# Moving attention and gate projections within the first layer's matmul order, with its bias and input loads, on one NeuronCore

## The chip, the cores and the metric

The kernel runs on one NeuronCore of a Trainium2 chip. The metric is the device time of one execution in microseconds (us). Before the change three runs gave a median of 3324.24 us, from 3323.4 to 3331.55.

## The reference

Two transformer-like layers over 512 tokens of width 1024, all in float32. The change lies wholly in the first part of the first one:

```python
h = rmsnorm(x, norm_mix_pre[i])
z = h @ w_in[i]
xr, gr, q, kc, vc, ksl, vsl, kw, vw, g_nsa, gm_rnn, gm_attn = jnp.split(z, IN_SPLITS, axis=-1)
xr = causal_conv(xr, conv_w[i], conv_b[i])
y_rnn = rg_lru(xr, ...) * jax.nn.gelu(gr)
kc_c = compress(kc.reshape(kv_shape), cmp_pos_k[i], cmp_k_w1[i], cmp_k_w2[i])
vc_c = compress(vc.reshape(kv_shape), cmp_pos_v[i], cmp_v_w1[i], cmp_v_w2[i])
y_attn = nsa(q, kc_c, vc_c, ksl..., vsl..., kw..., vw..., g_nsa, slopes)
y = jax.nn.sigmoid(gm_rnn) * y_rnn + jax.nn.sigmoid(gm_attn) * y_attn
x = x + rmsnorm(y @ w_out[i], norm_mix_post[i])
```

`rg_lru` is a gated linear recurrence over the tokens. `nsa` is attention with three branches: a softmax over 31 compressed blocks of keys, one over selected blocks and one over a window; with 512 tokens the last two are both plain causal attention here. After this come a feed-forward layer, an embedding term, and a second block with window attention and a mixture of experts, which the change leaves alone.

## The kernel before

Activations stand transposed: features on 128 partitions, 512 tokens along the free axis, eight such tiles for the width of 1024. One projection (`project`, L159) makes one output tile of 128x512 in one of PSUM's eight banks from eight matmuls. Each float32 matmul shows as two rows in the trace.

All weights come through a ring of six slots in SBUF (`Ring`). `chunk_list` gives the order of the chunks, some 2 MB each (1.5 MB for the recurrence). `feed` issues loads on SyncE's queue up to a given chunk; a load into a slot waits until the chunk that was there has been used (`used` names the semaphore). `take` makes an engine wait for the chunk's landing. Since SyncE issues in program order, everything behind a waiting load waits too.

The program is a row of blocks (`nc.Block`). In a block each engine has a list of instructions of its own, ordered by the code as written and synchronised by semaphores; at the block's end all engines meet at a barrier, SyncE too. The blocks that matter here, in order:

1. `norm_and_start`: SyncE loads x in two halves, two constants, and then feeds six chunks. Its next block, `rms_norms`, squares x on ScalarE, averages on TensorE, and scales on VectorE into H.
2. `recurrent_mixer`: for each of eight tiles three projections of H, and one tile later two gate matmuls (L301, L302) from VectorE's convolution. ScalarE and VectorE work on the recurrence of the tile. At the end TensorE has only the last two gate matmuls, and then ScalarE and VectorE finish the last tile.
3. `attention_inputs`: four projections for the compression's inputs (kc, vc), four for the keys, the values (L446), the 48 gate columns (L454), eight query projections, then the two compressions (L469), each over blocks that VectorE builds in one buffer (L549; the second build waits until the first product has read it), and the small second products.
4. `compressed_probs`: TensorE makes scores for four tiles (L584). VectorE adds a bias that SyncE loads piece by piece into two buffers, takes the maximum, ScalarE applies Exp, and VectorE masks, sums and scales (L603 to L625). TensorE turns the result (L591) and VectorE copies it (L629).
5. `causal_attention`: 32 units, pipelined over TensorE, VectorE and ScalarE. Its sixteen biases come into three buffers, the first three at its start (L702).
6. `mixer_output`: eight projections of H give the attention's gates; ScalarE applies Sigmoid (L846), VectorE multiplies and adds into Y; then eight projections of Y with w_out.

In 3, 4 and 6 the semaphore z_read counts what ScalarE has copied out of the banks, and TensorE waits for it before it writes a bank again.

## Time and profile before

| what | value |
|---|---|
| profiled execution, own time | 3322.41 us |
| its span | 3320.6 us |
| median of three runs | 3324.24 us (3323.4 to 3331.55) |
| TensorE busy | 2893.3 us, 87% of the span |
| VectorE busy | 1028.5 us, 31% |
| ScalarE busy | 673.2 us, 20% |
| moved by DMA | 635.62 MB, 191 GB/s on average |
| granted TensorE clock, mean | 0.932 |

The span runs from the first to the last instruction of the program; the execution's own time lies 1.8 us above it. Busy time says little by itself, since each stage has another limit. The views used below are: the timeline, which lists an engine's instructions in order of time, merged, with the start, the length and, in brackets, the idle time before and what ended it; windows, with the busy time of each engine in a stretch and the granted clock of TensorE (1.00 is 2.4 GHz, 0.50 is 1.2 GHz); and the landing time of DMAs. PE is TensorE, PEld its weight loads, DVE VectorE, ACT ScalarE, SP SyncE; a name with q behind it is that engine's sequencer, which at the end of a block means the barrier.

### The profile page before, as it was taken

The page shows a single profiled execution, that of the slowest core. Times are in us where ns is not written, and L with a number is a line of the kernel's source. Part 1 is how long each engine was busy: PE and PEld are TensorE (multiplying, and loading weights), DVE is VectorE, ACT ScalarE, POOL GpSimd, SP SyncE. Part 2 cuts the span into 40 slices and gives each one's busy share as a digit, 9 for nine tenths or more (in the row PEclk, how much of TensorE's full clock was granted, in tenths as well). Part 3 has the DMA queues.
Part 4 walks back from the last instruction along what each step waited for, and adds up shares of the span by engine and source line. Part 5 has one row for each costly group of instructions (what it writes and reads, how often), then busy time and mean ns, then how long its engine had stood idle before and what let it go on. Part 6 is the DMA issues. An engine that isn't in the chain of part 4 may idle for free. (4 is left out here: it accounts for less than half of the span.)

```text
span 3320.6 us, 37273 instructions
## 1 busy us (share of the span) xinstructions
PE 2893.3 (87%) x14080; PEld 1591.7 (48%) x14081; DVE 1028.5 (31%) x2150; ACT 673.2 (20%) x1368; POOL 123.5 (4%) x185
## 2 busy tenths in 40 slices
PE   6979878997999998898985989988678976999995
PEld 3435556543444443556653545444444643555543
DVE  2330066306788302125343111111322533111113
ACT  2440158311000000115331000000131631000002
POOL 0000000000000000000001001000100001110100
PEclk9989979998999998998996999999789997999997
DMA  4222210026665421111015999999712026999993
GB/s 168 94 80 89 85 53 27 29 76 171 263 228 213 180 82 38 63 51 58 25 54 202 396 406 410 420 401 410 286 50 96 1 82 256 397 391 415 396 403 116
DMA packets 139751, 635.62 MB, mean 191 GB/s; under 512 B 19366, under 2 KB 33062, under 8 KB 88576
## 3 DMA queue, kind: packets, MB, share of 16 engines
q1 hardware_dynamic: 95296, 422.13, 33.6%
q10 hardware_dynamic: 34992, 191.12, 14.3%
q0 software_dynamic: 9360, 21.00, 1.8%
q8 instruction: 65, 1.06, 0.1%
q14 instruction: 38, 0.31, 0.0%
HBM read 615.31 MB, written 37.22 MB: 197 GB/s over the span
## 5 line engine op out<-in xcount | busy, mean ns | idle before, releaser
L159 PE MATMUL psum<-normed,weight_ring 128*128 128x512 f32 x1472 | 642.2, 598 | 36.3 <-PEq L193 17.8
L159 PEld LDWEIGHTS psum<-normed,weight_ring 128*128 128x128 f32 x1472 | 282.5, 192 | 392.9 <-issue 392.9
L2079 PE MATMUL psum<-weight_ring,slot_rows_turned 128*64 128x256 f32 x3456 | 396.8, 383 | 0.9 <-issue 0.9
L2079 PEld LDWEIGHTS psum<-weight_ring,slot_rows_turned 128*64 128x64 f32 x3456 | 246.5, 138 | 146.6 <-issue 32.6
L2079 PE MATMUL psum<-third_stream_weights,slot_rows_turned 128*64 128x256 f32 x1728 | 217.5, 409 | 59.2 <-DMA third_stream_weights<-in_w_dram 59.2
L936 DVE SCALAR_TENSOR_TENSOR psum<-weight_ring,condition_rows 128x1024 f32<-128x1024 f32 x192 | 236.8, 1233 | 15.4 <-issue 0.9
L159 PE MATMUL psum<-modulated,weight_ring 128*128 128x384 f32 (+2 forms) x640 | 228.7, 518 | 0.0
L2079 PEld LDWEIGHTS psum<-third_stream_weights,slot_rows_turned 128*64 128x64 f32 x1728 | 130.3, 148 | 145.8 <-DMA third_stream_weights<-in_w_dram 66.5
L2094 PE MATMUL psum<-weight_ring,expert_hidden_turned 128*64 128x512 f32 x864 | 197.2, 598 | 0.0
L2211 DVE COPY expert_hidden_turned<-psum 128x256 f32<-128x256 f32 x81 | 34.4, 425 | 512.8 <-PE psum L2087 512.8
L2202 DVE COPY slot_rows_turned<-psum 128x512 f32<-128x512 f32 x81 | 56.1, 692 | 397.9 <-PE psum L2058 397.9
L159 PEld LDWEIGHTS psum<-modulated,weight_ring 128*128 128x128 f32 x640 | 121.4, 190 | 105.5 <-issue 51.0
L2155 ACT ACTIVATE expert_silu<-psum 128x256 f32<-128x256 f32 x79 | 30.3, 383 | 614.9 <-PE psum L2079 614.9
L159 PE MATMUL psum<-ffn_hidden,weight_ring 128*128 128x512 f32 x352 | 151.3, 592 | 0.9 <-issue 0.9
L159 PE MATMUL psum<-mix,weight_ring 128*128 128x512 f32 (+1 forms) x384 | 138.0, 521 | 2.2 <-PEq L1362 2.2
L2162 ACT COPY expert_rows<-psum 128x512 f32<-128x512 f32 x81 | 47.4, 585 | 325.2 <-PE psum L2094 325.2
L159 PEld LDWEIGHTS psum<-ffn_hidden,weight_ring 128*128 128x128 f32 x352 | 66.8, 190 | 85.4 <-issue 85.4
L2094 PEld LDWEIGHTS psum<-weight_ring,expert_hidden_turned 128*64 128x64 f32 x864 | 57.4, 136 | 99.1 <-issue 92.5
L159 PEld LDWEIGHTS psum<-mix,weight_ring 128*128 128x128 f32 x384 | 72.8, 190 | 66.7 <-issue 63.4
L2094 PE MATMUL psum<-third_stream_weights,expert_hidden_turned 128*64 128x512 f32 x432 | 98.7, 598 | 1.1 <-DVE expert_hidden_turned L2211 1.1
L1172 PE MATMUL psum<-weight_ring,modulated 128*128 128x384 f32 (+1 forms) x192 | 60.2, 478 | 26.2 <-PEq L1555 17.0
L2058 PE MATMUL psum<-identity,slot_rows 128*128 128x128 f32 x324 | 61.9, 315 | 21.9 <-DMA slot_rows<-token_rows,slot_index 20.1
(359 smaller groups left out, 2896.4 us busy)
## 6 DMA issues: line engine op xcount, KB each, us to landing
weight_ring<-in_w_dram SPq DMA_DIRECT2D x114, 2048.0 KB, 14.5
third_stream_weights<-in_w_dram ACTq DMA_DIRECT2D x81, 2048.0 KB, 18.7
weight_ring<-in_w_ada_dram SPq DMA_DIRECT2D x24, 2048.0 KB, 10.2
weight_ring<-in_w_ffn_dram SPq DMA_DIRECT2D x11, 2048.0 KB, 7.7
expert_rows<-expert_rows ACTq DMA_DIRECT2D x162, 128.0 KB, 12.7
weight_ring<-in_w_rnn_dram SPq DMA_DIRECT2D x8, 1536.0 KB, 14.5
weight_ring<-in_w_att_dram SPq DMA_DIRECT2D x6, 2048.0 KB, 7.6
weight_ring<-in_w_in_dram SPq DMA_DIRECT2D x6, 2048.0 KB, 9.5
```

The costliest lines, as they stand in the source:

```text
L159: last = nc.tensor.matmul(out, weights[:, k * P:(k + 1) * P], rhs(k), start=(k == 0), stop=(k == tiles - 1))
L936: last = nc.vector.scalar_tensor_tensor(out=product, in0=w[:, t], scalar=1.0, in1=CR[:, v, :], op0=ALU.mult, op1=ALU.mult, accum_out=c.mod ...
L1172: last = nc.tensor.matmul(ps[:, 4 + i % 2, 0:n], HX[:, k, i * P:(i + 1) * P], w[:, k, 0:n], start=(k == 0), stop=(k == KT - 1))
L2058: last = nc.tensor.transpose(ps[:, 0, k * P:(k + 1) * P], XS[:, b, k::4], c.ident[:, :])
L2079: last = nc.tensor.matmul(ps[64 * o:64 * o + 64, 2 + b, 256 * m:256 * (m + 1)], XT[:, b, k % 4, 64 * (k // 4):64 * (k // 4) + 64], w[:, k, ...
L2094: last = nc.tensor.matmul(ps[64 * o:64 * o + 64, 5 + b, :], HT[:, b, j % 2, 64 * (j // 2):64 * (j // 2) + 64], w[:, j, 512 * o:512 * (o + 1)],
L2155: nc.scalar.activation(SG[:, b, :], ps[:, 2 + b, 0:256], ACT.Silu).then_inc(silu.sem, 1)
L2162: nc.scalar.copy(YS[:, b, :], ps[:, 5 + b, :]).then_inc(y_copied.sem, 1)
L2202: v.tensor_copy(XT[:, b, :, :].rearrange("p k s -> p (k s)"), ps[:, 0, :]).then_inc(x_copied.sem, 1)
L2211: v.tensor_copy(HT[:, b, :, :].rearrange("p k s -> p (k s)"), ps[:, 1, 0:256])\
```

## The change

It does five things. The waits for both halves of x are put on SyncE ahead of the first ring loads. The four projections of chunk 8 (kc and vc) move from the head of `attention_inputs` into the end of the recurrence's block. The first compression moves between the two groups of four query projections, and the chunk order with it. Four of the eight gate projections move from `mixer_output` into `compressed_probs`, behind the scores; their sigmoids are written over their own weights in the ring slot, which stays in use until `mixer_output` has read it; the scores' banks now take the turned probabilities. The compressed bias is loaded in one piece into the place of the scores, and the first three causal biases are loaded in `compressed_probs`; the ring's next three loads go from `attention_inputs` to the head of `causal_attention`.

```diff
@@ norm_and_start, sync
                 for dst, src in c.const_loads:
                     sp.dma_start(dst, src).then_inc(c.consts_landed, 16)
+                for landed in c.x_landed:
+                    sp.wait_ge(landed, 16)
                 c.ring.feed(sp, Ring.SLOTS)
@@ recurrent_mixer, tensor, behind the loop
+                w = ring.take(pe).rearrange("p (s w) -> p s w", s=4)
+                for u in range(4):
+                    pe.wait_ge(z_read, 3 * KT - 5 + u)
+                    project(nc, ps[:, u, :], w[:, u], lambda k: H[:, k, :]).then_inc(c.att_z_ready, 1)
+                ring.used(c.att_z_ready, 4)
@@ attention_inputs, tensor
-                u = 0
-                for chunk in range(2):
-                    w = ring.take(pe).rearrange("p (s w) -> p s w", s=4)
-                    for s in range(4):
...
+                u = 4
+                w = ring.take(pe).rearrange("p (s w) -> p s w", s=4)
+                for s in range(4):
...
-                for b in range(2):
+                    b = chunk
                     w = ring.take(pe).rearrange("p (l n) -> p l n", l=16)
                     pe.wait_ge(xb_ready, b + 1)
@@ attention_inputs, sync
-                ring.feed(sp, 8 + 6)
                 sp.wait_ge(z_read, 4)
...
-                ring.feed(sp, ring.uses + Ring.SLOTS)
+                ring.feed(sp, ring.uses + 3)
@@ compressed_probs, sync
+                sp.dma_start(PC[:, :, :], c.ios["cmp_bias"]).then_inc(bias_in, 16)
                 sp.dma_start(MASK[:, :, :], c.ios["cmp_mask"]).then_inc(mask_in, 16)
-                for i in range(ST):
-                    if i >= 2:
-                        sp.wait_ge(bias_used, i - 1)
-                    sp.dma_start(BIAS[:, i % 2, :], c.ios["cmp_bias"][:, i, :]).then_inc(bias_in, 16)
-                    sp.wait_ge(bias_in, 16 * (i + 1))
+                for h in range(3):
+                    sp.dma_start(c.bias[:, h, :], c.ios["causal_bias"][h]).then_inc(c.bias_in[h], 16)
@@ compressed_probs, tensor
+                c.early_chunk = ring.uses
+                c.early_gates = ring.take(pe)
...
                     last.then_inc(s_ready, 1)
+                gates_w = c.early_gates.rearrange("p (s w) -> p s w", s=4)
+                for u in range(4):
+                    project(nc, ps[:, 4 + u, :], gates_w[:, u], lambda k: H[:, k, :]).then_inc(c.gm_ready, 1)
                 pe.wait_ge(p_ready, 1)
@@ compressed_probs, vector and scalar
-                    v.tensor_tensor(part, ps[:, i, :], BIAS[:, i % 2, :], ALU.add).then_inc(bias_used, 1)
+                    v.tensor_tensor(part, ps[:, i, :], part, ALU.add)
...
+                act.wait_ge(c.gm_ready, 4)
+                for u in range(4):
+                    nc.scalar.activation(c.early_gates[:, u * S:(u + 1) * S], ps[:, 4 + u, :], ACT.Sigmoid)
@@ causal_attention, sync
-                for h in range(NHEAD):
-                    if h >= 3:
-                        m_ready.wait(sp, ((h - 3) // 2 * UNITS + UNITS - 1) * 4 + (2 if (h - 3) % 2 == 0 else 4))
+                ring.feed(sp, c.early_chunk + Ring.SLOTS)
+                for h in range(3, NHEAD):
+                    m_ready.wait(sp, ((h - 3) // 2 * UNITS + UNITS - 1) * 4 + (2 if (h - 3) % 2 == 0 else 4))
@@ mixer_output, tensor and vector
-                for u in range(2 * KT):
+                for u in range(4, 2 * KT):
...
+                    gate = GA[:, u % 2, :] if u >= 4 else c.early_gates[:, u * S:(u + 1) * S]
...
+                ring.used(y_ready, 4, n=c.early_chunk)
@@ chunk_list
-    out += [tiles("w_att", 8, 4), tiles("w_att", 12, 4)]
-    out += [ios["cmp_k_w1"].rearrange("(l p) n -> p l n", p=P), ios["cmp_v_w1"].rearrange("(l p) n -> p l n", p=P)]
+    out += [tiles("w_att", 8, 4), ios["cmp_k_w1"].rearrange("(l p) n -> p l n", p=P)]
+    out += [tiles("w_att", 12, 4), ios["cmp_v_w1"].rearrange("(l p) n -> p l n", p=P)]
```

TensorE from the last gate matmuls of the recurrence to the second products of the compression, before (each row is a line of the kernel, the operation, its output and inputs and how often; a branch ends or begins a block):

```order
L302 MATMUL psum<-xr_conv,lru_gates_w 128x512
L278 UNCONDITIONAL_BRANCH
L431 UNCONDITIONAL_BRANCH
L159 MATMUL psum<-normed,weight_ring 128x512 x64
L446 MATMUL psum<-weight_ring,normed 128x512 x32
L454 MATMUL psum<-gate_columns,normed 128x48 x32
L159 MATMUL psum<-normed,weight_ring 128x512 x64
L469 MATMUL psum<-cmp_blocks,weight_ring 128x128 x64
```

The same place in the changed kernel:

```order
L304 MATMUL psum<-xr_conv,lru_gates_w 128x512
L159 MATMUL psum<-normed,weight_ring 128x512 x32
L280 UNCONDITIONAL_BRANCH
L438 UNCONDITIONAL_BRANCH
L159 MATMUL psum<-normed,weight_ring 128x512 x32
L452 MATMUL psum<-weight_ring,normed 128x512 x32
L460 MATMUL psum<-gate_columns,normed 128x48 x32
L159 MATMUL psum<-normed,weight_ring 128x512 x32
L475 MATMUL psum<-cmp_blocks,weight_ring 128x128 x32
L159 MATMUL psum<-normed,weight_ring 128x512 x32
L475 MATMUL psum<-cmp_blocks,weight_ring 128x128 x32
```

32 matmuls, four projections, now stand ahead of the block's end, and the first compression stands between the two halves of the query projections.

TensorE from the compressed scores to the causal attention, in the changed kernel; before, the row of L159 is not there and the other rows are the same:

```order
L587 MATMUL psum<-cmp_keys,queries 128x64 x32
L159 MATMUL psum<-normed,weight_ring 128x512 x32
L597 MATMUL psum<-identity,cmp_probs 128x128 x16
L570 UNCONDITIONAL_BRANCH
L712 UNCONDITIONAL_BRANCH
```

Four projections now stand between the scores and the transposes that wait for VectorE.

SyncE's DMAs from the end of `attention_inputs` on, in the changed kernel:

```order
L103 DMA weight_ring<-in_w_att_dram 128x4x1024 x2
L103 DMA weight_ring<-in_w_mix_out_dram 128x4x1024
L431 UNCONDITIONAL_BRANCH
L572 UNCONDITIONAL_BRANCH
L574 DMA cmp_probs<-in_cmp_bias_dram 128x2048
L575 DMA cmp_mask<-in_cmp_mask_dram 128x128
L577 DMA causal_bias<-in_causal_bias_dram 128x512 x3
L570 UNCONDITIONAL_BRANCH
L130 UNCONDITIONAL_BRANCH
L128 UNCONDITIONAL_BRANCH
L705 UNCONDITIONAL_BRANCH
L103 DMA weight_ring<-in_w_mix_out_dram 128x4x1024
```

Two more ring loads (w_ffn, w_ada) follow the last row, and then the thirteen other causal biases. Before, all three of these ring loads stood ahead of the first branch, and all sixteen causal biases behind the last.

## Rows read from the trace of the kernel before

**Rows 1.** Windows: a stretch, its length, busy us (instructions) by engine, granted clock, DMA share, GB/s.
```profile
414.00:448.20 34.20, 15.47 (x82) 14.91 (x82) 19.10 (x25) 3.75 (x5) 0.00 (x0) 0.53 0.24 85
```

**Rows 2.** Timeline of TensorE: start, length, line, operation, idle before and what ended it.
```profile
218.76 1.02 PE L302 MATMUL psum<-xr_conv,lru_gates_w 128*128 128x512 f32 x2
237.30 57.62 PE L159 MATMUL psum<-normed,weight_ring 128*128 128x512 f32 x128 [17.52 <-PEq L278]
...
387.63 7.31 PE L469 MATMUL psum<-cmp_blocks,weight_ring 128*128 128x128 f32 x64
402.23 9.21 PE L469 MATMUL psum<-cmp_blocks,weight_ring 128*128 128x128 f32 x64 [7.29 <-DVE cmp_blocks L549]
...
414.00 11.77 PE L584 MATMUL psum<-cmp_keys,queries 128*128 128x64 f32 x64 [1.03 <-PEq L424]
442.57 3.68 PE L591 MATMUL psum<-identity,cmp_probs 128*128 128x128 f32 x16 [16.80 <-DVE cmp_probs L625]
448.18 2.50 PE L713 MATMUL psum<-keys,queries 64*128 64x128 f32 x8 [1.93 <-PEq L128]
...
617.29 55.17 PE L159 MATMUL psum<-normed,weight_ring 128*128 128x512 f32 x128 [0.99 <-PEq L695]
674.73 56.87 PE L159 MATMUL psum<-mixed,weight_ring 128*128 128x512 f32 x128 [2.27 <-DVE mixed L856]
```

**Rows 3.** Timeline of all engines at the start.
```profile
8.93 7.11 SPq L103 DMA_DIRECT2D weight_ring<-in_w_rnn_dram  x1
16.52 1.28 ACT L203 ACT_TABLE_LOAD   x1 [16.39 <-PEq L168]
17.82 3.71 ACT L203 ACTIVATE x_squared<-residual 128x2048 f32<-128x2048 f32 x2
```

**Rows 4.** x's two loads and their landing; DMA until 8.9 us and until 16.04.
```profile
L174 SPq DMA_DIRECT2D residual<-in_xT_dram x2: 447/507/567, 1.3 to 1.8; - x2
DMA to landing us min/median/max: 5.3/6.5/7.8
...
DMA packets 2175, 2.14 MB, mean 241 GB/s; under 512 B 33, under 2 KB 2175, under 8 KB 2175
DMA packets 3061, 5.02 MB, mean 313 GB/s; under 512 B 80, under 2 KB 2384, under 8 KB 3061
```

**Rows 5.** Timeline of SyncE in another burst of six: its fourth issue, and its four middle ones.
```profile
2381.18 1.56 SPq L103 DMA_DIRECT2D weight_ring<-in_w_in_dram  x1
...
2380.01 7.85 SPq L103 DMA_DIRECT2D weight_ring<-in_w_in_dram  x4
```

**Rows 6.** Timeline of VectorE: its last operation in the recurrence.
```profile
236.22 0.69 DVE L385 TENSOR_TENSOR mixed<-lru_h,gelu_gr 128x512 f32<-128x512 f32 x1
```

**Rows 7.** Windows, cut where the granted clock changes.
```profile
237.30:242.24 4.94, 4.94 (x6) 2.16 (x7) 0.00 (x0) 0.00 (x0) 1.91 (x2) 0.50 0.36 73
416.32:426.00 9.68, 9.45 (x45) 9.26 (x44) 3.16 (x5) 0.63 (x1) 0.00 (x0) 0.50 0.43 153
...
442.50:460.69 18.19, 14.56 (x50) 10.18 (x50) 8.49 (x27) 6.64 (x21) 0.00 (x0) 0.50 0.14 44
```

**Rows 8.** Compressed softmax: SyncE's bias loads, their landing, VectorE's last copy.
```profile
414.35 13.79 SPq L575 DMA_DIRECT2D cmp_bias<-in_cmp_bias_dram  x4
...
DMA to landing us min/median/max: 3.1/3.2/7.2
...
446.28 0.69 DVE L629 COPY cmp_probs_turned<-psum 128x512 f32<-128x512 f32 x1 [0.16 <-PE psum L591]
```

**Rows 9.** Timeline of the causal attention's start: VectorE, SyncE, and the bias landings.
```profile
451.05 0.29 DVE L774 CUSTOM_DVE_ANT_0 causal_probs<-causal_bias,psum 128x128 f32<-128x128 f32 x1 [4.07 <-DMA causal_bias<-in_causal_bias_dram]
...
467.21 1.15 SPq L702 DMA_DIRECT2D causal_bias<-in_causal_bias_dram  x2
471.11 0.68 DVE L774 CUSTOM_DVE_ANT_0 causal_probs<-causal_bias,psum 128x512 f32<-128x512 f32 x1
DMA to landing us min/median/max: 2.6/2.8/4.0
```

**Rows 10.** Windows: the feed-forward stage's first products.
```profile
772.87:1077.85 304.98, 304.98 (x704) 134.61 (x704) 231.52 (x357) 16.29 (x24) 0.00 (x0) 0.99 0.69 238
```

48 lines of the change are left out of this document (24 added, 24 removed).

## The prediction, made before the changed kernel was run

> **What bounds the kernel now.** I read the windows by stage first, then TensorE's timeline with its waits, then the other engines around each wait, and last the granted clock. The change touches only the first 735 of 3320.6 us, so the question is what TensorE's path there loses and gains. From 37.8 us on TensorE works nearly all the time except in two stretches: 17.52 us behind the recurrence, ended by a barrier, and the compressed softmax from 414 to 448.2, where it is busy 15.47 of 34.2 us and waits 16.80 for VectorE in one piece [rows 1, 2]. A third wait, 7.29 us, is for the blocks of the second compression [rows 2]. The start is another kind: ScalarE waits 16.39 us, not for its input but for a barrier [rows 3]. What follows 735 us starts from a barrier or from work behind it, so what is won before is kept.
>
> **1. Inputs ahead of the weights.** ScalarE's first act is a table load at 16.52, and the squares follow at 17.82 [rows 3]; the two halves of x had landed long before: issued from 1.33 and 1.84, they took 5.3 and 7.8 us, the second thus at 9.64 [rows 4]. What ScalarE waited for was SyncE: a block ends for all engines when SyncE has issued its six ring loads, and the sixth issue alone took 7.11 us, from 8.93 to 16.04 [rows 3]. Nor did x wait for weights: by 8.9 us 2.14 MB had been moved, which is x and little else [rows 4]. So the edit does not bring x forward. It moves the six issues to 9.7 us and keeps them ahead of the same barrier. What it can gain is an emptier queue behind x. But when the sixth issue began, at 8.93, x was through already and what stood ahead of it was five loads of 1.57 MB, 7.9 MB; it ended when 5.02 MB had been moved in all, thus 2.8 MB of weights [rows 4]. In the changed kernel five issues at 0.48 us put the same 7.9 MB on the queue, of which about 0.4 MB leave before the sixth begins. A second burst of six on an empty queue, from 2379.6 us, had a long one too: its four middle issues took 7.85 us, the third of them 1.56, and one some 5.1 [rows 5]; 7.9 MB less 0.5 stood ahead of it. I therefore take a long sixth issue, by the shorter of the two: 9.7 + 2.4 + 5.1 = 17.2 instead of 16.04, **1.2 us lost**. Bounds: six issues at 0.48 us, 12.6, 3.4 won; a sixth of 7.1 us, 19.2, 3.2 lost. The first 1.5 MB then land near 9.7 + 7 = 17, well before TensorE asks for them at about 35, so the late weights cost nothing.
>
> **2. Four projections in the recurrence's tail.** TensorE's last gate product starts at 218.76 and VectorE ends the recurrence at 236.22 + 0.69 = 236.91; TensorE goes on at 237.30 [rows 2, 6]. Eight projections take 55.17 us at full clock [rows 2], so one is 6.87 and four are 27.5. Placed behind the last gate product they run from 219.7 to 247.2; ScalarE and VectorE need neither of them, their waits on ScalarE's reads (z_read) are met, and the chunk was loaded during the recurrence. The block now ends with TensorE at 247.2, about 10 us after the other engines, and the next four begin at 247.6. Before, the fourth projection ended at 237.30 + 27.5 + the half clock: the clock was 0.50 until 242.24 [rows 7], which cost half of 4.94, 2.5 us; 267.3 in all. Won: 267.3 - 247.6 = **19.7 us** (bounds: without the clock 17.2; without a new barrier gap 20.1). What moves behind this: the four copies of ScalarE come in one burst of 2.4 us, the swap's two DMAs are issued near 250, with the ring's load of the second compression's weights ahead of them; all are needed some 80 us later.
>
> **3. The compression between the query projections.** The first compression (7.31 us) now runs between two groups of four projections. VectorE's 16 block operations then have 27.5 us of cover where they had none, and need 7.3. So the 7.29 us wait before the second one goes. This second one took 9.21 where the first took 7.31 [rows 2]; I put that down to the clock after the idle time. Won: 7.29 + 1.9 = **9.2 us** (bounds 7.3 and 9.2). Its cover is the 27.5 us; nothing comes near it.
>
> **4. Gate projections in the compressed softmax, and gone from the mixer's output.** Removed there: four of eight, 27.5 us of TensorE at full clock. Added here, counted from the first score at T = 414.00: scores 11.77 us as before (from 416.32 on at half clock [rows 2, 7]), then 27.5 us, the first five of them at half clock as in the rows of part 2, 2.5 more: T + 41.8. VectorE is no bound: its first bias came 7.2 us after its issue, and the four went one after the other for 13.79 us [rows 8]; now one load of 1 MB with nothing ahead of it, for which the nearest rows are x's halves, 5.3 and 7.8 us [rows 4]. It would be through by about T + 24 to T + 27, against 28.6 before, and TensorE comes back only at T + 41.8. Then 16 transposes at full clock, half of 3.68 us, with VectorE's four copies (4 x 0.75) behind them: T + 45.2; ScalarE's four sigmoids at 0.60 end at T + 44.3 beside it. The gap from VectorE's last copy at 446.28 + 0.69 to TensorE's 448.18 is 1.2 us [rows 2, 8] and stays: T + 46.4 against T + 34.2. Sum: 27.5 - 12.2 = **15.3 us won**. Bounds: scores wholly at full clock save half of the 9.45 us that they ran at half [rows 7], and with no ramp 2.5 more, 7.2 in all; a ramp twice as long, 2.5 less. The masks, causal biases and the moved ring loads lie on SyncE, which has nothing else there.
>
> **5. Causal biases a stage ahead.** VectorE's first causal operation waited 4.07 us for its bias, until 451.05 [rows 9], while TensorE's scores had begun at 448.18. With the biases there, it could go about 0.6 us after TensorE, some 3.3 us sooner for the chain of the first unit. Against it stand an Exp table load that is new at this place (the sigmoids come between), and three 2 MB ring loads that SyncE now issues first. A table load is 1.28 us and the next activation starts right at its end (16.52 to 17.82 [rows 3]); it starts at the barrier, beside TensorE's and VectorE's first 1.0 us, and costs 0.3. The ring loads are 6.3 MB, some 15 us at the 0.41 MB a us at which weights moved in the start's rows (2.9 MB in 7.1 us [rows 4]); the fourth bias, issued at 467.21, 19.1 us in, and needed at 471.11 [rows 9], would now be issued about 16 us in, just behind them, and has 1.1 us to spare beyond the 2.8 that it takes. Net **3.0 us won** (bounds 0.5 and 3.3). The Trainium skill (ScalarE: Activation LUTs, What ACT_TABLE_LOAD costs) prices a switch of tables at 2.66 us, of which 1.38 is a drain behind the load. By that rule this term would be 1.6 and the forecast 1.4 us later; the row shows no such drain between load and use.
>
> **Sum**: -1.2 + 19.7 + 9.2 + 15.3 + 3.0 = 46.0 us. The profiled execution took 3322.4 us, so the changed one would take 3276.4; the median of the runs shown is 1.8 us above the profiled one. I say **3276**.
>
> **The rivals.**
> *The start comes forward.* The sixth issue passes in about 1.3 us, as the one of 1.56 did with some 5.7 MB ahead of it [rows 5]: the barrier comes at 13.4, term 1 is 2.6 won, the time 3273. For it: 7.5 MB ahead and not 7.9. Against: both bursts of six in this trace had one long issue. Chance 0.30.
> *The clock stays low in the compressed softmax.* Scores of 64 columns pulled it to half at 416.32 although TensorE was busy, and it stayed until 460.69 [rows 7]. If the four projections ran wholly at half clock they would cost 27.5 - 2.5 = 25 us more: 3301. Against: after 237.30 the same products brought it back in 4.94 us [rows 7]. Chance 0.08.
> *The clock stays full there*, the scores packed closer to dense work: 7.2 us less, 3269. Chance 0.06.
> *Slower.* TensorE now works from about 35 us to the causal stage without a rest over 2 us. If a sustained load drew the clock to its lower level in the feed-forward stage, its 304.98 us [rows 10] would double: 3276 + 305 = 3581. It decides from 46 us of this stage's present work on: at half clock these cost 46 us more, the whole gain, and 56 make the kernel slower by over 0.3%. Against: that stage held 0.99 for 305 us without a break [rows 10]. Chance 0.02.
>
> **How the numbers follow.** The forecast has 0.53. Bounds: the low end takes 4.6 more at the start, 7.2 at the scores and 0.3 in the causal stage, 3264; the high end 2.0 less at the start and 2.5 less in each of terms 2, 4 and 5, 3286. These hold the forecast and two of the rivals, some 8 to 9 in 10. About 0.3%, or 10 us, is what a measurement of this kernel can tell from no change. Only the slower rival (0.02) and an unforeseen 0.01 are not faster by more: 0.97, 0.01, 0.02.
>
> **What would show it.** In the changed profile: ScalarE's table load at about 17.7 us instead of 16.52, with one long issue before it (near 13.9 the first rival holds); TensorE busy without a break through the recurrence's end, with the next block about 0.4 us behind; both compressions at about 7.3 us with no wait between; four projections behind the scores in 30 us (over 45 the clock rival), transposes with no wait for VectorE; no wait on the causal biases; and four projections in the mixer's output, still with the 2.27 us wait before the second product [rows 2]. The prediction is wrong if a new wait over 3 us stands at one of these places, or if the feed-forward stage takes another time than 305 us.

## The result, and the profile after

The changed kernel took 3281.26 us (median of 4 runs, 3280.05 to 3284.92), beside 3325.52 us for the kernel before (3323.4 to 3331.55): 44.3 us less, a ratio of 0.9866 with a 95% interval of 0.9849 to 0.9883. The forecast was 3276 in a range of 3264 to 3286. The profiled execution of the changed kernel took 3281.26 us with a span of 3279.4, so the two profiles differ by 41.15 us of span, where the sum of the prediction was 46.0. The interval of the ratio stands for 39 to 50 us.

The first view is TensorE's timeline of the changed kernel. Its columns are start, length, line, operation, count, and the idle time before it with what ended it.

```profile
222.95 27.63 PE L159 MATMUL psum<-normed,weight_ring 128*128 128x512 f32 x64
251.51 27.70 PE L159 MATMUL psum<-normed,weight_ring 128*128 128x512 f32 x64 [0.93 <-PEq L280]
...
306.52 9.84 PE L460 MATMUL psum<-gate_columns,normed 128*128 128x48 f32 x64
...
346.11 7.31 PE L475 MATMUL psum<-cmp_blocks,weight_ring 128*128 128x128 f32 x64
353.25 27.63 PE L159 MATMUL psum<-normed,weight_ring 128*128 128x512 f32 x64
380.72 7.31 PE L475 MATMUL psum<-cmp_blocks,weight_ring 128*128 128x128 f32 x64
...
390.58 11.96 PE L587 MATMUL psum<-cmp_keys,queries 128*128 128x64 f32 x64 [1.03 <-PEq L431]
402.33 29.68 PE L159 MATMUL psum<-normed,weight_ring 128*128 128x512 f32 x64
431.86 1.91 PE L597 MATMUL psum<-identity,cmp_probs 128*128 128x128 f32 x16
436.16 4.53 PE L721 MATMUL psum<-keys,queries 64*128 64x128 f32 x16 [2.39 <-PEq L128]
...
602.65 27.70 PE L159 MATMUL psum<-normed,weight_ring 128*128 128x512 f32 x64 [0.99 <-PEq L703]
632.63 55.17 PE L159 MATMUL psum<-mixed,weight_ring 128*128 128x512 f32 x128 [2.27 <-DVE mixed L866]
```

Against [rows 2] the three holes are gone. Where TensorE stood 17.52 us behind the recurrence there is a burst of four projections and then 0.93 us; both compressions take 7.31 us and neither waits; the scores are followed at once by four projections, and the transposes that had waited 16.80 us for VectorE wait for nothing. The mixer's output has 64 products and not 128 ahead of its second product, with the same 2.27 us wait.

The same landmarks as a ledger, from the timelines of both profiles. "Gain" is how much earlier the changed kernel is at that place, "step" what was won or lost since the line above.

| TensorE's place | before, us | after, us | gain | step |
|---|---|---|---|---|
| first product of the block of the recurrence | 37.83 | 40.81 | -2.98 | -2.98 |
| last gate product | 219.19 | 222.52 | -3.33 | -0.35 |
| first product of the values | 294.76 | 279.05 | 15.71 | +19.04 |
| first small product behind the compressions | 411.92 | 388.50 | 23.41 | +7.70 |
| first causal score | 448.18 | 436.16 | 12.02 | -11.39 |
| mixer's output, first product | 617.29 | 602.65 | 14.64 | +2.62 |
| its second product (mixed) | 674.73 | 632.63 | 42.10 | +27.46 |
| feed-forward, first product | 772.87 | 726.92 | 45.95 | +3.85 |
| feed-forward, second product | 1078.75 | 1032.02 | 46.73 | +0.78 |
| second block, first product | 1337.97 | 1290.38 | 47.59 | +0.86 |
| end | 3320.55 | 3279.40 | 41.15 | -6.44 |

The two steps of the gate projections belong together: 27.46 less 11.39 is 16.07 us. So by the place where the change ends it had won 42.10 us. Two things were not in the sum at all: 5.49 us more from there to the second block (3.85 of them in the Y product and the norms), and 6.44 us lost in the second block, whose instructions the change does not touch. Both are looked at below, with the unchanged kernels.

At the start, SyncE's and ScalarE's timelines answer to [rows 3]. First SyncE's six ring loads, and the sixth by itself:

```profile
9.69 8.64 SPq L103 DMA_DIRECT2D weight_ring<-in_w_rnn_dram  x6
12.60 5.73 SPq L103 DMA_DIRECT2D weight_ring<-in_w_rnn_dram  x1
```

Then ScalarE:

```profile
18.81 1.28 ACT L205 ACT_TABLE_LOAD   x1 [18.67 <-PEq L168]
20.10 3.71 ACT L205 ACTIVATE x_squared<-residual 128x2048 f32<-128x2048 f32 x2
```

The burst begins at 9.69, as forecast from the landing of x's second half, and ends at 18.33; the barrier follows. Its first five issues took 2.91 us, where the forecast had 2.4, and the sixth 5.73, where it had 5.1. ScalarE's wait is again for a barrier, now of 18.67 us, and the squares follow the table load by 1.29 us, at 20.10.

In the causal stage's start ScalarE, VectorE and SyncE read so:

```profile
436.11 1.28 ACT L809 ACT_TABLE_LOAD   x1 [1.99 <-PEq L128]
437.41 0.40 ACT L809 ACTIVATE causal_probs<-causal_probs,causal_max 128x128 f32<-128x128 f32 x1
```

```profile
396.87 0.69 DVE L609 TENSOR_TENSOR cmp_probs<-psum,cmp_probs 128x512 f32<-128x512 f32 x1 [36.16 <-DMA cmp_probs<-in_cmp_bias_dram]
412.29 2.29 DVE L631 TENSOR_TENSOR cmp_probs<-cmp_probs,cmp_stats 128x2048 f32<-128x2048 f32 x1
...
436.77 0.29 DVE L782 CUSTOM_DVE_ANT_0 causal_probs<-causal_bias,psum 128x128 f32<-128x128 f32 x1 [1.80 <-PE psum L721]
...
455.56 0.69 DVE L782 CUSTOM_DVE_ANT_0 causal_probs<-causal_bias,psum 128x512 f32<-128x512 f32 x1 [0.50 <-DMA causal_bias<-in_causal_bias_dram]
```

```profile
390.54 0.35 SPq L574 DMA_DIRECT2D cmp_probs<-in_cmp_bias_dram  x1
```

VectorE's first causal operation waits for TensorE's scores, 1.80 us, and no longer for a bias, 4.07 us in [rows 9]. The fourth bias, behind the three ring loads now, is waited for once, for 0.50 us. The Exp that follows the new table load starts 1.30 us after it. In the compressed softmax the one load of 1 MB is issued at 390.54 and the first addition starts at 396.87, 6.3 us later; VectorE is through at 414.58. Counted from T, the start of the first score, that is T + 24.0, and not T + 28.5 as in the kernel before.

Last, stretches cut where the granted clock changes (a stretch, its length, busy us and instructions by engine, clock, DMA share, GB/s), of the changed kernel:

```profile
306.52:310.78 4.26, 4.26 (x40) 4.26 (x39) 0.00 (x0) 0.59 (x1) 0.00 (x0) 1.00 0.70 222
310.78:321.02 10.24, 10.24 (x33) 7.52 (x33) 0.00 (x0) 0.00 (x0) 0.00 (x0) 0.50 0.28 114
...
392.70:406.35 13.65, 13.65 (x52) 11.43 (x52) 8.19 (x13) 2.72 (x5) 0.00 (x0) 0.50 0.32 126
```

TensorE is busy for the whole of each of them, and in two the clock stands at the lower level (1.2 GHz). Both times it fell while products of 48 or 64 columns ran: the gate columns from 306.52 and the scores from 390.58.

### The profile page after: what moved, and what is told of

Its sections match the earlier page's. It is cut to its first block and busy times, and to the rows that moved or that the text cites. A ratio compares the mean times of both kernels' runs of the same rounds, so it can differ in the third digit from the quotient of the medians.

```text
span 3279.4 us, 37267 instructions
## 1 busy us (share of the span) xinstructions
PE 2883.5 (88%) x14080; PEld 1585.0 (48%) x14081; DVE 1027.8 (31%) x2150; ACT 675.5 (21%) x1370; POOL 124.6 (4%) x185
## 5 line engine op out<-in xcount | busy, mean ns | idle before, releaser
L159 PE MATMUL psum<-normed,weight_ring 128*128 128x512 f32 x1472 | 642.5, 598 | 19.8 <-PEq L195 17.8
L159 PEld LDWEIGHTS psum<-normed,weight_ring 128*128 128x128 f32 x1472 | 282.4, 192 | 375.1 <-issue 375.1
L947 DVE SCALAR_TENSOR_TENSOR psum<-weight_ring,condition_rows 128x1024 f32<-128x1024 f32 x192 | 236.9, 1234 | 15.3 <-issue 0.9
L159 PE MATMUL psum<-modulated,weight_ring 128*128 128x384 f32 (+2 forms) x640 | 228.7, 518 | 0.0
L159 PEld LDWEIGHTS psum<-modulated,weight_ring 128*128 128x128 f32 x640 | 121.4, 190 | 105.5 <-issue 51.0
L159 PE MATMUL psum<-ffn_hidden,weight_ring 128*128 128x512 f32 x352 | 151.3, 592 | 0.9 <-issue 0.9
L159 PE MATMUL psum<-mix,weight_ring 128*128 128x512 f32 (+1 forms) x384 | 139.5, 526 | 2.2 <-PEq L1373 2.2
L159 PEld LDWEIGHTS psum<-ffn_hidden,weight_ring 128*128 128x128 f32 x352 | 66.8, 190 | 85.4 <-issue 85.4
L159 PEld LDWEIGHTS psum<-mix,weight_ring 128*128 128x128 f32 x384 | 73.4, 192 | 67.6 <-issue 64.3
```

Of the source, the lines that this page charges most:

```text
L159: last = nc.tensor.matmul(out, weights[:, k * P:(k + 1) * P], rhs(k), start=(k == 0), stop=(k == tiles - 1))
L947: last = nc.vector.scalar_tensor_tensor(out=product, in0=w[:, t], scalar=1.0, in1=CR[:, v, :], op0=ALU.mult, op1=ALU.mult, accum_out=c.mod ...
```

## The experiments

What they had to settle: whether the start's loss is the wait for x or the burst of six; whether the three moves are worth alone what the ledger gives them; how term 4's 16.07 us divide between projections and the bias load; what the causal biases bring; and whether the 6.44 us lost in the second block belong to the change. The kernel before was timed again beside each group of runs; ratios are to it, with their 95% interval.

**The wait for x taken out** (from the changed kernel):

```diff
-                for landed in c.x_landed:
-                    sp.wait_ge(landed, 16)
                 c.ring.feed(sp, Ring.SLOTS)
```

> The changed kernel without SyncE's two waits for x. Theory (the barrier behind the sixth ring load gates ScalarE, and x is never late): the six loads are issued from about 4.4 us again, the sixth ends near 16, ScalarE's table load starts at 16.5 instead of 18.8, the last gate product of the recurrence at 218.8 instead of 222.1, and the kernel takes 3278, 3.3 us less than the changed one. Rival (x does arrive sooner when the weights wait, and that helps): ScalarE's start gets later than 18.8 or the first product starts later than 40.8, the kernel takes 3281 or more.

It took 3276.03 us, 0.9839 [0.9822, 0.9855], with a span of 3276.2, 3.2 below the changed kernel's profile. SyncE's and ScalarE's timelines:

```profile
4.38 11.94 SPq L103 DMA_DIRECT2D weight_ring<-in_w_rnn_dram  x6
```

```profile
16.80 1.28 ACT L203 ACT_TABLE_LOAD   x1 [16.67 <-PEq L168]
```

The start is back where [rows 3] had it, within 0.3 us, with 2.0 us won at the table load and 2.08 at TensorE's first product (38.73 against 40.81). The wait only pushes the burst back. The burst takes 8.64 us instead of 11.94 when it starts later: 1.9 us less in the first five issues and 1.4 in the sixth (5.73 and not 7.11). But the shorter span does not come from these 2.08 us. By the second block's first product this profile was 1.25 us behind the changed kernel's (1291.63 against 1290.38): 1.65 us more had gone in the causal stage and 1.7 in the mixer's first projections. Only the second block made it shorter, with 1984.6 us and not 1989.0. Nor do the intervals of the two ratios tell the kernels apart.

**One load fewer in the burst** (from the kernel before):

```diff
-                c.ring.feed(sp, Ring.SLOTS)
+                c.ring.feed(sp, Ring.SLOTS - 1)
```

> The kernel before with five ring loads ahead of the first barrier instead of six; the sixth is issued by the recurrence's own feed at about 30 us. Theory (the sixth issue alone is stuck, since the queue is full): SyncE is through at 8.9 us, ScalarE's table load starts near 9.4, the first half of x is in at 6.6, so the squares start near 10.7 instead of 17.8; the first product starts at 30.7 instead of 37.8 and the kernel takes 3318, 7 us less than before. Rival (any last load is stuck, or the barrier is not what ScalarE waits for): the table load stays at 16.5 and the kernel at 3325.

It took 3316.6 us, 0.9967 [0.9955, 0.998], which stands for 7 to 15 us less. SyncE, then ScalarE:

```profile
4.35 4.67 SPq L103 DMA_DIRECT2D weight_ring<-in_w_rnn_dram  x5
```

```profile
9.49 1.28 ACT L203 ACT_TABLE_LOAD   x1 [9.36 <-PEq L168]
```

The sixth issue alone held every engine for the 7.0 us between 9.49 and 16.52, and 7.10 us of it reached TensorE's first product (30.73 against 37.83), as expected. That is the cause of the start, and the change leaves it in place.

**The burst issued behind the barrier** (from the changed kernel, without the wait for x):

```diff
-                for landed in c.x_landed:
-                    sp.wait_ge(landed, 16)
-                c.ring.feed(sp, Ring.SLOTS)
...
+        if first:
+            @block.sync
+            def _(sp):
+                c.ring.feed(sp, Ring.SLOTS)
```

> The changed kernel without the waits for x, and with the six ring loads issued in the norm's block, so that no barrier stands behind them. Theory (ScalarE waited for the barrier alone): the table load starts near 5 us, the squares near 6.7 when the first half of x lands, the first product near 26.7 instead of 40.8, 14 us won, and the first weights, in at 14 us, are no bound; kernel 3267. Rival (the weights then bound the start, or x and the weights collide): the first product waits for weights or x lands over 1 us later, under 8 us won, 3273 or more.

It took 3268.22 us, 0.982 [0.9804, 0.9837]. SyncE and ScalarE:

```profile
4.80 11.42 SPq L103 DMA_DIRECT2D weight_ring<-in_w_rnn_dram  x6
```

```profile
4.81 1.28 ACT L207 ACT_TABLE_LOAD   x1 [4.68 <-PEq L168]
6.82 1.91 ACT L207 ACTIVATE x_squared<-residual 128x2048 f32<-128x2048 f32 x1 [0.72 <-DMA residual<-in_xT_dram]
9.85 1.91 ACT L207 ACTIVATE x_squared<-residual 128x2048 f32<-128x2048 f32 x1 [1.12 <-DMA residual<-in_xT_dram]
```

The burst is about as long as without the wait, 11.42 us, but no barrier stands behind it. Now ScalarE does wait for x, 0.72 and 1.12 us. TensorE's first product starts at 27.62, 13.2 us before the changed kernel's 40.81, and 13.09 us of it are still there at the second block's first product.

**The tail alone** (the kernel before, with four projections moved into the recurrence's block):

```diff
+                w = ring.take(pe).rearrange("p (s w) -> p s w", s=4)
+                for u in range(4):
+                    pe.wait_ge(z_read, 3 * KT - 5 + u)
+                    project(nc, ps[:, u, :], w[:, u], lambda k: H[:, k, :]).then_inc(c.att_z_ready, 1)
+                ring.used(c.att_z_ready, 4)
```

> The kernel before with nothing but the four projections moved into the recurrence's tail. Theory: 19.0 us won as in the changed kernel's trace (values start 275.7 instead of 294.8: 17.5 of idle time less the new gap at the barrier, 0.5 to 0.9, and 2.5 of half clock), the kernel takes 3306. Rival (part of the gain is only shifted and comes back at the next stage): less than 12 us are won by the start of the compressed softmax.

It took 3309.15 us, 0.9938 [0.9921, 0.9955]. TensorE's timeline, and below it the stretch in which its 64 scores ran:

```profile
221.54 27.63 PE L159 MATMUL psum<-normed,weight_ring 128*128 128x512 f32 x64
250.10 27.70 PE L159 MATMUL psum<-normed,weight_ring 128*128 128x512 f32 x64 [0.93 <-PEq L278]
```

```profile
398.95:406.30 7.35, 7.33 (x64) 7.19 (x64) 0.00 (x0) 1.24 (x1) 0.00 (x0) 1.00 0.72 283
```

The values' first product comes at 277.64, 17.12 us earlier than before, although the last gate product came 1.9 us later in this profile: 19.0 us for the move, as in the ledger. The gap of 0.93 us is there again. By the first score 2.1 us had been lost, 1.7 of them because the clock stood at the lower level for 10.24 us from the gate columns on and not for 6.83, and 0.4 in the second compression. So 15.05 us were won at the start of the compressed softmax, where the rival had less than 12. By the second block's first product 14.58 were left, and then its second block took 1991.3 us where the first profile of before has 1982.6. The scores ran at full clock here, in 7.33 us and not 11.77, and VectorE, the bound of that stage, was waited for all the longer.

**The interleaved compression alone** (from the kernel before, with the order of the weight chunks changed to match):

```diff
                     ring.used(z_ready, u)
-                for b in range(2):
+                    b = chunk
                     w = ring.take(pe).rearrange("p (l n) -> p l n", l=16)
```

> The kernel before with nothing but the first compression between the query projections. Theory: the 7.29 us wait goes and the second compression takes 7.31 instead of 9.21, 9.2 us won by the start of the compressed softmax (404.8 instead of 414.0); the kernel takes 3316. Rival (the lower clock sits elsewhere and stays): 7.3 us or less, the second compression still over 8 us.

It took 3316.66 us, 0.9969 [0.9957, 0.9982], which stands for 6 to 14 us less. In its profile the first score starts at 404.71 instead of 414.00: 9.29 us, the forecast's 9.2. TensorE's timeline:

```profile
360.23 7.31 PE L469 MATMUL psum<-cmp_blocks,weight_ring 128*128 128x128 f32 x64
367.38 27.63 PE L159 MATMUL psum<-normed,weight_ring 128*128 128x512 f32 x64
394.85 7.31 PE L469 MATMUL psum<-cmp_blocks,weight_ring 128*128 128x128 f32 x64
```

**The gate projections back in the mixer's output** (from the changed kernel; VectorE's and ScalarE's parts moved back with them):

```diff
-                gates_w = c.early_gates.rearrange("p (s w) -> p s w", s=4)
-                for u in range(4):
-                    project(nc, ps[:, 4 + u, :], gates_w[:, u], lambda k: H[:, k, :]).then_inc(c.gm_ready, 1)
                 pe.wait_ge(p_ready, 1)
...
-                for u in range(4, 2 * KT):
+                for u in range(2 * KT):
```

> The changed kernel with all eight gate projections in the mixer's output again; the single load of the compressed bias stays. Theory (the gain of this part is idle time filled, and of the 16.1 us that the trace shows for term 4 some 4.6 come from the bias, which no longer arrives in four steps): VectorE is through 24.0 us after the first score, the causal attention starts 29.6 us after it instead of 45.6, and the mixer's output takes 27.5 us more; 11.5 us lost, the kernel takes 3293. Rival (all of term 4 comes from the gates): the causal attention starts 34 us after the first score as before, 16 us lost, 3297.

It took 3297.0 us, 0.9901 [0.9881, 0.9921]. TensorE's timeline:

```profile
390.90 11.79 PE L585 MATMUL psum<-cmp_keys,queries 128*128 128x64 f32 x64 [1.03 <-PEq L431]
415.05 3.68 PE L592 MATMUL psum<-identity,cmp_probs 128*128 128x128 f32 x16 [12.36 <-DVE cmp_probs L626]
420.63 4.49 PE L713 MATMUL psum<-keys,queries 64*128 64x128 f32 x16 [1.91 <-PEq L128]
```

From the first score to the causal stage it takes 29.73 us; before it was 34.18, and in the changed kernel 45.58. So of term 4's 16.07 us, 4.45 come from the new bias load, which shortened TensorE's wait for VectorE from 16.80 to 12.36 with no projection moved, and 11.6 from the projections. Two things stand behind the 4.45. VectorE's four additions no longer wait for one load each (0.96, 0.83 and 1.04 us before). And the first addition comes 6.38 us after the first score and not 7.62; before, a 2 MB ring load had been issued 2.9 us ahead of the bias, and here it comes later, in the causal stage. No run parts this ring load from the one load in place of four. In time the kernel took just what the rival had, 3297, but the causal stage began 29.73 us after the first score, as the theory had it, and not 34; the ratio's distance from the changed kernel's, 0.0035, is 11.6 us, with intervals too wide to tell it from 16. Its second product in the mixer's output starts 12.25 us later than the changed kernel's, which bears that out. By the feed-forward stage the distance was 16.06: the norms between took 98.1 us here and 94.3 there. That last step is the one dealt with under the unchanged kernels below.

**The causal biases late** (from the changed kernel, the first three loaded in their own stage, ahead of the ring's loads):

```diff
-                for h in range(3):
-                    sp.dma_start(c.bias[:, h, :], c.ios["causal_bias"][h]).then_inc(c.bias_in[h], 16)
...
+                for h in range(3):
+                    sp.dma_start(BIAS[:, h, :], c.ios["causal_bias"][h]).then_inc(bias_in[h], 16)
                 ring.feed(sp, c.early_chunk + Ring.SLOTS)
```

> The changed kernel with the first three causal biases loaded at the head of the causal stage again, ahead of the three ring loads. Theory (VectorE waited for them): VectorE's first causal operation comes 2.9 us after TensorE's first score instead of 0.6, the second waits again, and 2.5 to 3.3 us are lost by the end of the first unit; kernel 3284. Rival (the first unit waits for the clock, and the biases matter little): under 1 us lost, kernel 3281 to 3282.

It took 3286.03 us, 0.9873 [0.9856, 0.9889]. VectorE's timeline:

```profile
438.36 0.29 DVE L782 CUSTOM_DVE_ANT_0 causal_probs<-causal_bias,psum 128x128 f32<-128x128 f32 x1 [3.55 <-DMA causal_bias<-in_causal_bias_dram]
```

The wait for the bias is back, 3.55 us. TensorE's first product of the compressed attention starts at 447.51 and not 444.76: 2.75 us, and 2.4 at the mixer's output. The ratios, 0.9873 and 0.9866, don't tell the two kernels apart; what is shown is shown by the trace.

**The gap behind the tail closed** (from the kernel with the burst behind the barrier): the recurrence issues one ring load fewer, and the next block issues it ahead of its first wait.

```diff
-                ring.feed(sp, ring.uses + Ring.SLOTS)
+                ring.feed(sp, ring.uses + Ring.SLOTS - 1)
...
+                ring.feed(sp, 8 + 7)
                 sp.wait_ge(z_read, 4)
```

> As the one above, and the load of the second compression's weights is issued in the next block instead of at the end of the recurrence's, where SyncE waits for TensorE's last projection, issues, and only then reaches the barrier. Theory: the gap on TensorE between the two blocks falls from 0.93 to about 0.4 us, another 0.5 us won, 3266.5, which the times alone cannot tell; the trace shows the gap. Rival (the gap is TensorE's own drain): it stays at 0.9.

It took 3269.6 us, 0.9827 [0.981, 0.9843]; the kernel it starts from took 3268.22. TensorE's timeline:

```profile
237.64 6.67 PE L159 MATMUL psum<-normed,weight_ring 128*128 128x512 f32 x15 [0.44 <-PEq L282]
```

So 0.49 of the 0.93 us is SyncE's issue at the block's end, and 0.44 the barrier. In time it brought nothing: in the causal stage the clock stood at the lower level for 13.65 us from 423.61, where the kernel it starts from had 3.41. The stage took 170.19 us and not 166.47, 3.7 us more.

**Both kernels once more, unchanged.** First the kernel before:

> The kernel before, unchanged, profiled once more. Theory (the changed kernel won 47.6 us up to the second block, and the 6.4 us that its profiled execution lost from there to the end are the spread of a stage that the change leaves alone): from the second block's first product to the end this run takes another time than the 1982.6 us of the first one, by several us, within the 1982 to 1991 of all profiled kernels so far. Rival (the change itself slows the experts' stage): within 1 us of 1982.6 again.

It took 3326.92 us, 0.9999 [0.9986, 1.0012]. Its span was 3325.0, 4.4 longer than the first profile's, and its second block took 1989.1 us and not 1982.6. Then the changed kernel:

> The changed kernel, unchanged, profiled once more. Theory as in the run above: the stretch from the second block's first product to the end differs from its first 989.0 + 1000 = 1989.0 us by several us, the stretch before it by less than 2, unless the granted clock falls at another place. Rival: 1989 again, with the kernel before at 1982.6 again.

It took 3280.7 us, 0.9857 [0.9833, 0.988], and its second block 1989.4 us beside 1989.0: here the expected difference of several us did not come. The waits of TensorE in the second block, summed, show a part of it; the first row of that view for the first profile of before, for the changed kernel and for before again:

```profile
PE psum L2079 <- DMA third_stream_weights<-in_w_dram: 59.2, 17, 6.2
```

```profile
PE psum L2090 <- DMA third_stream_weights<-in_w_dram: 63.0, 16, 6.4
```

```profile
PE psum L2079 <- DMA third_stream_weights<-in_w_dram: 61.0, 15, 5.9
```

The columns are us in total, times, longest. The experts' weights come 59.2, 63.0 and 61.0 us late in sum: 3.8 of the 6.4 us between the two kernels, but only 1.8 of the 6.5 between the two profiles of the kernel before. The rest of it was not traced. With the same kernel before at 1982.6 and 1989.1 us, and all 14 profiles between 1982.6 and 1991.3, the 6.44 us of the ledger lie within what an unchanged program does. The norms between the mixer's output and the feed-forward stage are the same kind: with the Y product they took 98.1 and again 94.2 us before, 94.3 and again 96.6 after, and from 94.2 to 98.1 over all the profiles. From the Y product to the second block the kernel before took 663.2 and again 657.6 us.

Set against each other, these two profiles give the ledger a second time. At the second product of the mixer's output 47.45 us are won, where the first pair gave 42.10, and at the second block's first product 43.14 and not 47.59. By terms, the second pair has -1.46 at the start, 19.22 for the tail, 7.81 for the compression, 17.67 for the gate projections and 4.21 for the causal biases. So two pairs of profiles of the same two kernels differ by up to 1.9 us in one term and by 5.35 in the sum.

**The gate columns spread** (from the kernel with the burst behind the barrier): each of the four groups of 16 products of 48 columns runs behind one of the four values' products, not all 64 in a row.

```diff
                 w = ring.take(pe).rearrange("p (k n) -> p k n", k=KT)
+                pe.wait_ge(small, 32)
                 for i in range(ST):
...
                     u += 1
-                ring.used(z_ready, u)
-                pe.wait_ge(small, 32)
-                for i in range(ST):
                     for k in range(KT):
...
                 last.then_inc(gates_ready, 1)
+                ring.used(z_ready, u)
```

> The kernel with the ring loads behind the barrier, and the 64 short products of the gate columns set four ways between the products of the values, instead of in one run of 9.8 us. Theory (the clock fell to half because TensorE did little in each step there, not because it rested): no half clock between 293 and 310 us, the columns take 8.9 us or less in all and the four query projections behind them 27.5 instead of 30.0; about 3.5 us won by the first compression, kernel 3264.7. Rival (the clock falls anyway, by its own rhythm): the half-clock stretch stays, nothing won, 3268.

It took 3262.83 us, 0.9817 [0.9792, 0.9842]. TensorE's timeline, then the stretch of all eight pieces:

```profile
265.84 7.03 PE L455 MATMUL psum<-weight_ring,normed 128*128 128x512 f32 x16
272.71 1.88 PE L460 MATMUL psum<-gate_columns,normed 128*128 128x48 f32 x16
274.42 7.10 PE L455 MATMUL psum<-weight_ring,normed 128*128 128x512 f32 x16
281.36 1.88 PE L460 MATMUL psum<-gate_columns,normed 128*128 128x48 f32 x16
```

```profile
265.84:300.20 34.36, 34.36 (x128) 19.05 (x126) 0.00 (x0) 2.93 (x5) 0.00 (x0) 1.00 0.18 62
```

The clock held 1.00 all through, where the same products in one row had drawn it to 0.50 for 10.24 us. The first score starts at 372.39, 5.06 us before that of the kernel it starts from (377.45), and 4.98 of it were won between the values and the first compression, where 3.5 were expected. The low stretch at this place was there in all twelve profiles with the columns in one row, and in neither of the two with the columns spread. By the second block's first product 2.36 us were left, and the ratios, 0.9817 and 0.982, don't tell this kernel from the one it starts from: the gain is shown by the trace, at its place, and not by the times.

**The scores spread too** (from that one): the groups of scores and the gate projections alternate in the compressed softmax.

```diff
+                gates_w = c.early_gates.rearrange("p (s w) -> p s w", s=4)
                 for i in range(ST):
...
-                for u in range(4):
-                    project(nc, ps[:, 4 + u, :], gates_w[:, u], lambda k: H[:, k, :]).then_inc(c.gm_ready, 1)
+                    for u in ((0,), (1,), (), (2, 3))[i]:
+                        project(nc, ps[:, 4 + u, :], gates_w[:, u], lambda k: H[:, k, :]).then_inc(c.gm_ready, 1)
```

> As the one above, and the compressed scores set between the gate projections (score, projection, score, projection, two scores, two projections). Theory: the clock stays full through this stage too, TensorE is through with both about 34.5 us after the first score instead of 41.3, VectorE, whose last score comes at 21 us, needs until about 34 and is just no bound; 6 us won, kernel 3259. Rival (VectorE becomes the bound, since its scores come later): the transposes wait for it over 3 us, and under 4 us are won.

It took 3263.24 us, 0.981 [0.9781, 0.9838]. The stretches:

```profile
372.12:378.95 6.83, 6.83 (x21) 4.76 (x22) 0.47 (x1) 1.09 (x1) 0.00 (x0) 0.50 0.78 278
378.95:409.99 31.04, 31.04 (x110) 16.64 (x109) 15.78 (x21) 3.80 (x5) 0.00 (x0) 1.00 0.00 1
```

The lower level lasted 6.83 us and not 13.65, and from the first score to the transposes it took 38.0 us and not 41.25: 3.2 us won there, where 6 were expected. The rival's cause did not come either: VectorE was through at 408.07, and the transposes, at 409.99, waited for nothing behind the last projection. The clock fell just at the first score all the same (372.12, with the first score at 371.97), before anything had been spread. The two medians, 3262.83 and 3263.24, are not told apart. Both versions beat both kernels; the better stands some 18 us below the changed kernel and 64 below the one before.

## Why the prediction was right, point by point

The time, 3281.26, lies in the range and 5 us above the forecast; the sign and the order of the parts were right. None of the four rivals came: the start did not come forward, the clock did not stay low through the compressed softmax's projections (29.68 us for four, where four at full clock take 27.63), it did not stay full there, and the feed-forward stage took 304.20 us.

**Term 1, inputs ahead of the weights: -1.2 forecast, -3.33 measured.** The mechanism is as put: x never waited for weights, and SyncE's burst ahead of the barrier set the start. The size was off by 1.1 us at the table load, since the burst took 8.64 us and not 2.4 + 5.1 = 7.5. The five issues ahead took 2.91 and not 2.4. The sixth took 5.73: of the two long issues that the trace showed, 5.1 and 7.1, the shorter was taken, which was a fifth issue and not a sixth, and this one was between them. That is inside the bound of 3.2 at the table load. On TensorE another 0.69 us went because the products for the mean square took 9.83 us and not 9.14, at a granted clock of 1.00 in both; the kernel before took 9.84 for them when it was run again, so no edit is needed for that. The last 0.35 went at the recurrence's first projections, where the lower clock lasted 3.7 us and not 3.0. In the second pair of profiles the term was -1.46, near the forecast.

**Term 2, the tail: 19.7 forecast, 19.04 here and 19.0 alone.** The barrier's gap was put at 0.4 and measured 0.93. What the step left out is SyncE's ring load at the end of the recurrence's block; without it the gap was 0.44. It also left out what the move costs behind it, which shows in term 3.

**Term 3, the compression: 9.2 forecast, 9.29 alone, 7.70 in the changed kernel.** The move itself was right to 0.1 us. What failed is the silent assumption that the work between stays as it was: the gate columns took 9.84 us and not 8.85, and the query projections behind them lost 0.68, because the clock stood low for 10.24 us there and not for 6.83. The profiles show whose cost this is. With the columns in one row, all eight profiles with the four projections in the recurrence's tail have the long stretch, the one with the tail alone among them, and all four without them the short one, the one with the interleaving alone among them. So about 1.6 us of what the tail brings are lost here each time, and the interleaving has no part in it. Why the stretch is longer then stays open.

**Term 4, the gate projections: 15.3 forecast, 16.07 measured.** The step's T + 46.4 was T + 45.58, and the projections' 30 us were 29.68. But the text gave VectorE's earlier end no worth, since TensorE came back last. Set against a kernel that has the new bias load and not the projections, they bring 11.6 us, and the load 4.45. The sum was right to 0.8 us; its reason was short of one part. The second pair of profiles gave 17.67, of which 1.6 are low clock in the mixer's output of the kernel before.

**Term 5, causal biases: 3.0 forecast, 2.62 measured** to the mixer's output. At TensorE's first product of the compressed attention it was 4.11, of which putting the biases back took 2.75. The other 1.4 go with the clock, which before stood low for the first 12.5 us of the stage (until 460.69 [rows 7]) and here for 3.4; no run shows it by itself. Later in the stage the clock stood low twice, and once before, which took 1.5 back. So that the term came out at its forecast is in part luck: the second pair gave 4.21. The stage took 169.05 to 170.39 us in the six profiles with the biases late, 165.57 to 168.14 in seven of the eight with them early, and 170.19 in the eighth. Nor had the fourth bias the 1.1 us to spare that the step gave it: VectorE waited 0.50 us for it. The table load cost what [rows 3] said: by the rule of the Trainium skill (ScalarE: Activation LUTs, What ACT_TABLE_LOAD costs), 1.38 us of drain would stand behind it, and the Exp started at 437.41, at the load's end. The trace does not agree with that figure here.

**What the sum did not have.** "What is won before is kept" is where the two profiles differ most from the forecast. From the Y product to the second block 5.49 us came on top, and 6.44 went in the second block, -0.95 in all. Run again unchanged, the kernel before moved by 5.6 us in the first of these stretches and by 6.5 in the second, without any edit. So no cause in the change is needed for either. The forecast's 46.0 lies between the 42.10 and the 47.45 of the two pairs, and an agreement of the sum to better than some 5 us is luck. The medians, 44.3 apart, with an interval of 39 to 50, bear 42.10 out as well as 46.0.

## What to carry to other kernels

When all engines wait at a start, ask which engine the barrier waits for, and whether its last act is needed before the barrier at all: six weight loads behind the barrier, and no wait for the inputs ahead of them, were worth 13.2 us at TensorE's first product, of which the wait alone was 2.1. Before crediting a move with a whole gap, take away in thought whatever else the same edit does to that gap (here the new bias load, with a ring load no longer ahead of it, had shortened it by 4.45 us). And where the clock falls in a row of products with few columns, try mixing dense ones between them, and read the gain at its place: it brought 5.0 us at the gate columns and 3.2 at the scores, and neither was clear in the kernel's time. Last, profile the unchanged kernel twice before reading a ledger: here its stages moved by up to 6.5 us.

## What the runs showed of the hardware

SyncE took 0.4 to 0.5 us to issue the first weight load of a burst. At the start, behind five other loads of 1.57 MB, the sixth issue took 7.11 us in each burst that began between 4.3 and 4.9 us, ahead of a barrier or behind it, and 5.6 to 5.8 in each that waited for x and began at 9.6 us or later; five issues without a sixth took 4.67. A burst of six later in the kernel before, with loads of 0.5 to 2.1 MB, had its long issue too, but it was the fifth, 5.08 us, and the sixth took 1.08. No run shows what an issue waits for.

The granted clock fell to its lower level while TensorE was busy 100% of the time, in rows of products with 48 and 64 columns, and did not fall when 16 products with 48 columns stood between groups of 16 with 512: 34.36 us at 1.00. It does not fall in every such row: in the kernel with the tail alone the 64 scores ran at 1.00, with TensorE busy 7.33 of 7.35 us. The length of a low stretch at one place differed between kernels with the same instructions there (6.83 or 10.24 us at the gate columns, 3.41 or 13.65 in the causal stage), and gains of 1 to 4 us at one place were given back at the next in that way.

The barrier behind the recurrence cost TensorE 0.44 us, and 0.93 where SyncE still had one load to issue ahead of it.
